# A merge in two half passes, one product drawn ahead of the second half, and the output rows split half by half

## The reference, cut to what matters

```python
merged = jax.nn.sigmoid(g_a) * y_a + jax.nn.sigmoid(g_b) * y_b
x = layer_norm(ALPHA * x + merged @ w_out[i], ln2_g[i], ln2_b[i])
x = layer_norm(ALPHA * x + 0.5 * swiglu(x, ffn2_w1[i], ffn2_w3[i], ffn2_w2[i]),
               ln3_g[i], ln3_b[i])
...
cat = jnp.concatenate([ya * jax.nn.silu(za), yb * jax.nn.silu(zb),
                       yc * jax.nn.silu(zc), yd * jax.nn.silu(zd)], axis=-1)
return jnp.einsum('bte,ed->btd', cat, lp['w_out']), h_final
```

## Time and profile before

| | us |
|---|---|
| median of three runs | 3362.88 (3362.01 to 3364.14) |
| the profiled execution, its own time | 3362.1 |
| its span in the profile | 3360.2 |
| TensorE busy (matmul) | 3260.7 |
| VectorE busy | 1889.2 |
| ScalarE busy | 1087.2 |
| moved by DMA | 249.05 MB, 74 GB/s on average |

### The profile page before, as it was taken

The page is one execution under the profiler, slowest core; times in us unless marked ns, Lnnn a source line. Parts: engine busy times, 40 slices in busy tenths (PEclk is TensorE's granted clock), DMA queues, the critical chain, the costliest instruction groups (busy, mean ns, idle before and its releaser), DMA issues.

```text
span 3360.2 us, 37265 instructions
## 1 busy us (share of the span) xinstructions
PE 3260.7 (97%) x15362; PEld 2649.8 (79%) x15362; DVE 1889.2 (56%) x3223; ACT 1087.2 (32%) x1572; POOL 2.2 (0%) x9
## 2 busy tenths in 40 slices
PE   8999999999999999988989999999999999999898
PEld 7888888877888777777868888888877687788687
DVE  4323323247759678878573332222387698789536
ACT  3121211225242446655142111111155533423412
POOL 0000000000000000000000000000000000000000
PEclk9999999999999999999999999999999999999999
DMA  3211111113333350002201111111111221122141
GB/s 145 84 63 60 66 57 63 63 44 112 106 97 132 129 194 10 7 26 107 106 32 51 51 57 44 51 44 51 51 63 50 94 76 64 44 73 94 69 163 69
DMA packets 88536, 249.05 MB, mean 74 GB/s; under 512 B 8496, under 2 KB 24240, under 8 KB 86832
## 3 DMA queue, kind: packets, MB, share of 16 engines
q1 hardware_dynamic: 88368, 246.68, 21.0%
HBM read 202.60 MB, written 44.04 MB: 73 GB/s over the span
## 4 chain that ended last, share of the span: by engine, by line
PE 88%; DVE 7%; ACT 3%; issue 1%; DMA 0%; DVEq 0%; SPq 0%; ACTq 0%
PE PS L375 87%; PE PS L380 2%; DVE X L1939 1%; DVE WS L1931 1%; DVE HELD L1971 1%; ACT PT L1113 1%; ACT WS L1113 1%; ACT TMP L1540 1%; DVE COLB L2606 0%; DVE PR L1931 0%; DVE XS L1939 0%; DVE PT L1931 0%; DVE HELD L1931 0%; DVE XS L1931 0%; ACT XS L1113 0%
## 5 line engine op out<-in xcount | busy, mean ns | idle before, releaser
L375 PE MATMUL PS<-XS,WS 128*128 128x512 f32 (+1 forms) x8400 | 1943.9, 392 | 21.7 <-DVE XS L1931 13.3
L375 PEld LDWEIGHTS PS<-XS,WS 128*128 128x128 f32 x8400 | 1574.6, 189 | 372.8 <-issue 35.2
L375 PE MATMUL PS<-HS,WS 128*128 128x512 f32 x2208 | 510.3, 391 | 0.7 <-DVE WS L1931 0.7
L375 PEld LDWEIGHTS PS<-HS,WS 128*128 128x128 f32 x2208 | 415.2, 188 | 90.9 <-issue 4.5
L1113 ACT ACTIVATE WS<-RAW 128x1024 fp32r<-128x1024 f32 x286 | 293.5, 1050 | 523.6 <-PE PS L375 461.1
L1931 DVE TENSOR_TENSOR TMP<-TMP,PS 128x512 f32<-128x512 f32 x112 | 76.5, 686 | 651.1 <-PE PS L375 644.4
L1931 DVE TENSOR_TENSOR WS<-RAW,WS 128x1024 fp32r<-128x1024 f32 x286 | 342.8, 1220 | 109.4 <-ACT WS L1113 109.1
L1113 ACT ACTIVATE TMP<-PS 128x512 f32<-128x512 f32 x184 | 109.0, 596 | 524.0 <-PE PS L375 520.4
L1939 DVE SCALAR_TENSOR_TENSOR X<-PS,X 128x512 f32<-128x512 f32 x160 | 109.9, 689 | 240.5 <-PE PS L375 240.2
L1113 ACT ACTIVATE HS<-TMP 128x512 fp32r<-128x512 f32 x88 | 55.6, 632 | 481.4 <-DVE TMP L1931 481.4
L1939 DVE SCALAR_TENSOR_TENSOR CV<-UU,COL,CV 128x1024 f32<-128x1024 f32 x120 | 154.0, 1283 | 3.4
(11 more groups left out here) (294 smaller groups left out, 2786.1 us busy)
## 6 DMA issues: line engine op xcount, KB each, us to landing
RAW<-in_W SPq DMA_DIRECT2D x290, 512.0 KB, 3.6
DC<-TMP SPq DMA_DIRECT2D x32, 256.0 KB, 2.0
X<-in_xT SPq DMA_DIRECT2D x8, 512.0 KB, 8.6
DX<-X SPq DMA_DIRECT2D x2, 2048.0 KB, 8.2
DCZ<-CA SPq DMA_DIRECT2D x8, 512.0 KB, 4.0
DGA<-TMP SPq DMA_DIRECT2D x16, 256.0 KB, 2.6
DGB<-TMP SPq DMA_DIRECT2D x16, 256.0 KB, 3.6
CZ<-DCZ SPq DMA_DIRECT2D x8, 512.0 KB, 6.0
```

The lines of the kernel that those rows point to most:

```text
L375: done = d.matmul(out, l, r, start=first, stop=last)
```

## The change

Merge: the eight rows of h = 0 come first, then the eight of h = 1 in the order 3, 4, 5, 6, 7, 0, 1, 2. Rows 3 to 7 keep their slots; rows 0, 1 and 2 are loaded and split a second time, so the list W has three units more (293 for 290) and the numbers in `loads(...)` rise by three.

Feed-forward: the first product of fi = 2, its w1 for h = 0, is made before the second half of fi = 0 and 1. Its unit takes the fifth slot.

Outputs: rows are split in halves of 512, the first half as soon as the zc product (3, 0) is done; the two rows that come by DMA come in two DMAs of 512 KB. In `c_norm` the squares' second product with ones comes one product earlier, both roots stand together (two table loads fewer) and so do both silu and copy steps.

```diff
+MERGE = [(m, 0) for m in range(8)] + [(m, 1) for m in (3, 4, 5, 6, 7, 0, 1, 2)]
...
+    def ab_row(k, h):
+
+        return RW[:, k, half(h)] if k < 6 else XSf[:, 1, k, half(h)]
...
-            def up(fis):
-                us = {fi: (w.take(), w.take()) for fi in fis}
+            def up(fis, ahead=None, done=None):
+
+                us = {fi: (w.take() if done is None else done, w.take()) for fi in fis}
+                one_more = None
...
+                        early = done is not None and h == 0
+                        if not early:
+                            banks.take(use1, (ac, name, "silu", fi, h))
...
+                        if not early:
+                            product8(us[fi][0], h, use1, tag, within=first)
...
+                    if ahead and h == 0:
+                        one_more, use1 = w.take(), (name, "up1", ahead, 0)
+                        banks.take(use1, (ac, name, "silu", ahead, 0))
+                        product8(one_more, 0, use1, tag, within=None)
+                return one_more
...
-                product8(u, h, use, "mh", pair=mh_pair, beside=h == 1, within=m in (3, 5) and h == 1 or None)
...
+                product8(u, h, use, "mh", pair=mh_pair, beside=h == 1, within=m in (3, 6) and h == 1 or None)
+            us = [w.take() for _ in range(8)]
+            us += us[3:] + [w.take() for _ in range(3)]
+            for i, (u, (m, h)) in enumerate(zip(us, MERGE)):
+                if i == 8:
                     side = merge_norm(0)
+                out_product(u, m, h)
+                if u not in us[i + 1:]:
+                    release(u)
             flush()
             side = merge_norm(1)
...
                     act(ZC[:, m, half(h)], bank("zc", m, h), ACT.Silu).then_inc(*ac.inc("zc", m, h))
+                    if m == 3:
+                        cat_rows(h)
                 release(u)
+
+        def cat_rows(h):
+
+            for k in range(8):
+                e.wait_ge(dma("rw")("rw"), mm("zc", 3, h), *([dma(f"rows{h}")("rows")] if k > 5 else ()))
+                act(XS[:, 0, k, half(h)], ab_row(k, h), ACT.Copy).then_inc(*ac.inc("xs", "ab", k, h))
...
+                u = w.take()
+                if m < 3:
+                    release(u)
+            for h in range(2):
+                for k in range(8):
+                    e.wait_ge(ac("xs", "ab", k, h))
+                    low(XS[:, 1, k, half(h)], ab_row(k, h), XS[:, 0, k, half(h)]).then_inc(*ve.inc("xs", "ab", k, h))
+            release(u)
...
             squared(0)
-            for _ in range(3):
+            yield
+            yield
+            squared(1)
+            for h in range(2):
+                root("c", h, 512, LN_EPS, mm("sq", "c", h, 3))
                 yield
-            squared(1)
-            scaled(0)
-            for _ in range(2):
+            for h in range(2):
+                scaled(h)
                 yield
-            scaled(1)
-            yield
...
-        e.wait_ge(*[cat_in(row, h) for row in (6, 7) for h in range(2)], mm("zc", 3, 1))
-        d.dma_start(XSf[:, 1, 6:8, :], DC[6:8].rearrange("k p n -> p k n")).then_inc(*dma("rows0").inc("rows"))
+        for h in range(2):
+            e.wait_ge(cat_in(6, h), cat_in(7, h), mm("zc", 3, h))
+            d.dma_start(XSf[:, 1, 6:8, half(h)], DC[6:8].rearrange("k p n -> p k n")[:, :, half(h)]).then_inc(
+                *dma(f"rows{h}").inc("rows"))
...
-    w += [(u, "split") for u in by_m(i["w_out"][0])]
+    w_out = by_m(i["w_out"][0])
+    w += [(u, "split") for u in w_out + w_out[:3]]
```

More of the change, by code:

```diff
@@ L496, in ffn @@
             for fi in range(22):
-                if fi != 1:
-                    up([0, 1] if fi == 0 else [fi])
+                if fi == 0:
+                    more = up([0, 1], ahead=None if with_mod else 2)
+                elif fi > 1:
+                    up([fi], done=more if fi == 2 else None)
                 if with_mod and fi:
@@ L1595, in merge @@
             nonlocal side
-            for m in range(3):
-                release(w.take())
-            us = [w.take() for _ in range(5)]
+            us = [w.take() for _ in range(8)]
+            us += us[3:] + [w.take() for _ in range(3)]
+            for u in us[:3]:
+                release(u)
             side = norm("ln2", 0, mm("ya", 7, 1))
-            for m in range(3, 8):
-                hook()
-                release(us[m - 3])
+            for i, u in enumerate(us[8:]):
+                if i in (0, 1, 3, 4, 5):
+                    hook()
+                release(u)
             flush()
@@ L1819, in scaled @@
                 for k in range(4):
-                    e.wait_ge(ac("cs", h, k), ve("xs", "ab", 5, 0))
+                    e.wait_ge(ac("cs", h, k), ve("xs", "ab", 5, 1))
                     act(CVH[:, k, half(h)], CV[:, k, half(h)], ACT.Copy).then_inc(*ac.inc("csh", h, k))
             squared(0)
-            for _ in range(3):
+            yield
[3 more added lines that the diff above has]
+                root("c", h, 512, LN_EPS, mm("sq", "c", h, 3))
                 yield
-            squared(1)
-            scaled(0)
-            for _ in range(2):
+            for h in range(2):
+                scaled(h)
                 yield
-            scaled(1)
-            yield
         def outputs():
             nonlocal side
[L1835 to L1841, removed]
             def ab_pass(ms):
@@ L2692, in out_product @@
                 stt(x, x, ALPHA, bank("wo", m, h), ALU.mult, ALU.add).then_inc(*ve.inc("wo", m, h))
[L2693 to L2703, removed]
-                for _ in range((2, 0, 1, 1, 1)[m - 3]):
+                order = [k for k, g in MERGE if g == h]
+                norm_add("ln2", order.index(m), h, XA, x_now, ve("cxy", 7), order)
+            us = [w.take() for _ in range(8)]
+            us += us[3:] + [w.take() for _ in range(3)]
+            for i, (u, (m, h)) in enumerate(zip(us, MERGE)):
+                if i == 8:
+                    side = norm("ln2", 0, XA, x_now)
+                for _ in range((2, 0, 0, 1, 1, 1, 0, 0)[i - 8] if h else 0):
                     hook()
-                out_product(m, 1)
-                release(us[m - 3])
+                out_product(m, h)
+                if u not in us[i + 1:]:
+                    release(u)
             flush()
@@ L3015, in outputs @@
             x_in = {}
-            for k in range(8):
-                x = RW[:, k, :] if k < 6 else XSf[:, 1, k, :]
-                e.wait_ge(ac("xs", "ab", k, 0))
-                low(XS[:, 1, k, :], x, XS[:, 0, k, :]).then_inc(*ve.inc("xs", "ab", k, 0))
-                ve.same("xs", "ab", k, 1)
             def gated_add(use):
@@ L3360, in sync @@
             x_back(k)
-        loads(277)
+        loads(280)
         for m in range(4):
@@ L3365, in sync @@
             if m % 2:
-                loads(278 + m // 2)
-        loads(282)
+                loads(281 + m // 2)
+        loads(285)
         e.wait_ge(ve("cp", 3, 1))
@@ L3370, in sync @@
             x_back(k)
-        e.wait_ge(*[cat_in(12 + k, h) for k in range(4) for h in range(2)], ac("xs", "ab", 5, 0), ve("xs", "ab", 5, 0))
+        e.wait_ge(*[cat_in(12 + k, h) for k in range(4) for h in range(2)], ac("xs", "ab", 5, 1), ve("xs", "ab", 5, 1))
         d.dma_start(ACf[:, 1], DC[12:16].rearrange("k p n -> p k n")).then_inc(*dma("sg").inc("sg"))
-        loads(286)
+        loads(289)
         e.wait_ge(*[cat_in(8 + k, h) for k in range(4) for h in range(2)], mm("ab", 4, 1))
         d.dma_start(XSf[:, 1, 0:4, :], DC[8:12].rearrange("k p n -> p k n")).then_inc(*dma("rows2").inc("rows"))
-        loads(290)
+        loads(293)
         for p in range(3):
```

33 lines of the change are left out of this document (10 added, 23 removed).

## The result

The changed kernel takes **3330.69 us** (median of 4 runs, 3330.51 to 3333.28), the kernel before, beside it on the same chip, 3363.51. The ratio is 0.9905, 95% interval 0.9888 to 0.9922: 32.8 us less, with some 26 to 38 inside the interval. The forecast was 3330.8, from a kernel before at 3362.88. The profiled execution's span is 3328.7 us, 31.5 less than before's.

The account below looks back on a forecast made before the run. TensorE, 88% of the last-ending chain, was taken as the bound, losing time to idleness and a slower clock. Gains of 16.2 (seam) and 15.9 us (outputs) sum to 32.1, off the median 3362.88: forecast 3330.8 us, range 3326 to 3341.

Parts of the forecast that it names:

- Where the time is: Seam and start of outputs: TensorE waits for VectorE, 8.4 and 4.5 us, then 4.1 and 6.2 us.
- Seam, gain 16.2: Seam of merge and second feed-forward: 10.7 us earlier, with one product of 5.44 us already done.
- of the loss 2.6 stays: Seam: of the 18.8 us lost there before, 2.6 us would remain after the change.
- the prediction's sign: Seam: up1(0, 1) would wait for XS row by row, 2 to 3 us in all.
- The clock taken as full: Seam: the sub-microsecond gaps between rows k would not lower TensorE's clock; cost chosen as 0 us.
- The bound of 2.1: Seam: if the short gaps between rows counted as idleness, the end would be 2.1 us later.
- Outputs, gain 15.9: Start of the outputs: half rows and the norm's new order would save 15.9 of 16.3 us lost.
- the two losses: Time lost before the change: 18.8 us at the seam, 16.3 us at the outputs; 34.9 together.
- Rows late: Outputs: second half's rows land 3 us late beside loads of X, plus clock; time 3336; chance 0.13.
- VectorE the bound at the seam: Seam: VectorE, with 0.3 us to spare, becomes the bound, costing 5 to 9 us; time 3338; chance 0.09.
- Only one place pays: Seam or outputs: the change at one doesn't work or its wait returns; time 3347; chance 0.05.
- Weights set the merge's pace: Merge, first pass: reloads queue behind XA, which would have to be 47 us late; time 3370; chance 0.02.

Follow-up runs that it names:

- e3: The changed kernel with the merge back in its old order, product drawn ahead and new outputs kept: 3339.60 us.
- e2: The changed kernel without the feed-forward product drawn ahead: 3336.90 us.
- e5: The changed kernel with A's and B's rows split whole and one 1 MB transfer, c's norm in its new order: 3337.78 us.
- e4: The changed kernel with the norm of c back in its old order on all three engines, half rows kept: 3339.50 us.
- e6: The changed kernel with six more repeated weight splits on VectorE ahead of the sum of h = 1: 3338.89 us.
- e7: The changed kernel with the remaining norm steps of h = 1 moved ahead of up(1,0)'s silu and product on ScalarE and VectorE: 3328.63 us.
- e1: The changed kernel with merge and second feed-forward as before the change, only the outputs new: 3345.43 us.
- e8: The changed kernel with the outputs as before the change, only merge and second feed-forward new: 3348.70 us.
- e9: The changed kernel itself, unaltered, measured again on another chip: 3332.15 us, against 3361.91 for the kernel before.
- e10: The norm-first kernel (remaining norm steps of h = 1 ahead of up(1,0)'s silu and product) measured again beside the changed kernel: 3329.83 us.

## Why the prediction was right

The time came within 0.1 us of the forecast and each place within 0.6 of its term; that the whole is closer than its parts is luck. The traces show 31.3 us saved where the sum has 32.1, the kernel before measured 3363.51 here and not 3362.88, and the same two kernels on another chip gave 3332.15 and a difference of 29.8 instead of 32.8.

- **Where the time is.** Two places, four waits for VectorE: right. Each of the four has been brought back or kept alone (8.3 in e3, 4.5 in e2, 4.1 in e5, 6.2 in e4), and beyond its idle time each cost 1.6 to 3.0 us more, most of it for the clock.
- **Seam, gain 16.2.** Measured 15.7 from the mean to the row behind up3(0, 1), 15.6 up to zc's last silu, with either outputs. The steps: VectorE at the mean of h = 0, 1675.57 for 1675.7; the sum of h = 1 ready 1719.47 for 1719.6; TensorE there 1719.85 for 1719.9; the margin 0.38 for 0.3; the chain of h = 1 32.5 long, as said, ended at 1753.41 for 1753.5. The reciprocal of h = 0 waited 0.21 us for ScalarE where 0.4 was allowed. Oversized by half a us: of "of the loss 2.6 stays" the size was 3.1 (18.8 - 15.7); up3(0, 1) came 10.45 earlier, not 10.7, from a mean that was 0.15 earlier too. The waits between rows k (0.56, 0.39, 0.40) hold 1.35 of the 3.1, where the prediction's sign was 2 to 3 us of them; the rest isn't placed.
- **The clock taken as full.** Right: 1.00 in each window, with gaps of 0.18, 0.56, 0.39 and 0.40. The bound of 2.1, which would have followed from the Trainium skill (TensorE: Matmul & The Clock Gate, What's actually happening) if gaps so short counted as idleness, wasn't needed. That the throttled state comes back where activity stops agrees with e2, where the same place with a wait of 4.51 shows 0.70 behind it; behind a wait of 3.0 us, told of in the last section, it came back in half of the traces.
- **Outputs, gain 15.9.** Measured 15.7 to 16.2 by the stretches. The half rows took ScalarE 3.22 us for six (0.54 each) and VectorE 3.70 (0.62), as reckoned. The wait for TMP was 0.24, within 0.2 to 0.4. A mis-sized term is the landing of half a MB: 4.1 us, not 3.5. ScalarE did wait for both, in its timeline:

```profile
3112.54 1.15 ACT L1124 ACTIVATE XS<-XSf 128x512 fp32r<-128x512 f32 x2 [0.32 <-DMA XSf<-DC]
3113.94 0.60 ACT L1124 ACTIVATE ZC<-PS 128x512 f32<-128x512 f32 x1 [0.25 <-PE PS L380]
...
3118.16 1.15 ACT L1124 ACTIVATE XS<-XSf 128x512 fp32r<-128x512 f32 x2 [0.51 <-DMA XSf<-DC]
```

  TensorE waited for neither itself, but the second left its mark. The copy of a weight stands behind it on ScalarE, VectorE's split of that weight waited 0.17 us for it, and from there VectorE's queue has no gap up to the squares' sum: 0.17 of TensorE's 0.24. The rule on the fixed part of a DMA that the rival cited (the Trainium skill, DMA: Bandwidth & Descriptors, Anatomy of one DMA) agrees in kind only: two halves take 4.1 us each against 4.8 for the whole in e5, where its formula, an estimate for another path of issue, gives 3.2 and 4.4. The measured times decide.
- **Slips of the sum.** The outputs' work is 43.5 + 3.5 - 0.2 = 46.8 us, not 46.9, and the two losses make 35.1, not 34.9. Neither moves the forecast or its range by more than 0.2.
- **What the sum didn't say.** It gave the outputs one number over two cures. The text followed the new order of the norm of c in its times ("the second squares are summed by about 3151") but never priced it. That is how the expectations of e4 and e5, written later, could be wrong by 7 and 6 us while the prediction held: a total that comes out right doesn't say which part carries it.
- **The rivals.** Rows late: they were, by 0.3 and 0.5 us, and at most 0.17 of it reached TensorE. VectorE the bound at the seam: at the mean it misses that by 0.38 us, as e6 shows (behind the mean its chain is the bound, as e2 and e7 show), and the tally that left out its waits for ScalarE missed nothing large. Only one place pays: no (e1, e8). Weights set the merge's pace: no wait for WS at the seam.

## What to carry to other kernels

Price a change wait by wait, not place by place: ask of each wait which instruction stands ahead of the late one in its engine's queue, and take that part out alone before crediting it. When work moves to another half or another order, the small sums that another engine waits for (here three additions of 2.3 us in all) should go ahead of the long step of the half before them. And an edit of 2 us can be told by a stretch between two events of the trace where whole times spread by 2 to 4, as long as no wait of several us lies in the stretch: behind such a wait the clock can differ between executions.

## What the runs showed of the hardware

**TensorE's clock behind four waits.** Windows right behind four waits of TensorE: 4.51 us (e2), 4.12 (e5), 6.18 (e4), 7.06 (e6), one fence a kernel, and PEclk the third number from the end:

```profile
1748.30:1754.00 5.70, 5.69 (x18) 4.04 (x19) 3.27 (x5) 2.05 (x3) 0.00 (x0) 0.70 0.00 0
```
```profile
3120.50:3126.00 5.50, 5.31 (x15) 3.68 (x15) 5.50 (x6) 5.05 (x6) 0.00 (x0) 0.69 1.03 418
```
```profile
3150.90:3157.00 6.10, 6.08 (x13) 4.18 (x14) 3.87 (x2) 1.98 (x2) 0.00 (x0) 0.51 0.01 3
```
```profile
1727.30:1733.00 5.70, 5.67 (x11) 3.81 (x12) 4.64 (x7) 2.11 (x4) 0.00 (x0) 0.50 0.48 175
```

In each the window after it shows 0.98 to 1.00 again. 0.50 is 1.2 GHz of the two levels, 0.70 a stretch part at 1.2 and part at 2.4. What each kernel lost beyond its added waits was 1.65 us in e2 (5.6 less 3.95), 2.5 in e5 (7.0 less 4.5), 3.0 in e4 (9.3 less 6.3) and 2.1 in e6 (8.2 less 6.1): the price isn't proportional to the wait. Nor does one wait have one price: the same 6.16 us cost 0.6 more in e8 than in before. The gaps of up to 0.56 in the change stand beside a clock of 1.00.

**The same wait, another clock.** Nine traces with the new merge reach its first mean between 1672.81 and 1677.16 us, though nothing ahead of it differs; e2 and e7, on one chip, lie 4.0 apart. In the four whose waits up to there were compared, TensorE's waits differ by a us or two, one way and the other. A part of the spread is the clock. Between 800 and 900 us the change's first trace has 1.00, its second (e9) 0.98, with TensorE busy 97.0 us in both and 397 matmuls against 390. By windows of 4 us all of it lies behind one wait that both have, in TensorE's timelines and the windows behind it, first the first trace, then e9:

```profile
843.88 2.84 PE L380 MATMUL PS<-TMP,ones 128*128 128x512 f32 x6 [3.04 <-ACT TMP L1124]
844.00:848.00 4.00, 4.00 (x13) 2.29 (x14) 3.59 (x13) 2.84 (x4) 0.00 (x0) 1.00 0.35 147
```
```profile
843.38 4.33 PE L380 MATMUL PS<-TMP,ones 128*128 128x512 f32 x6 [3.03 <-ACT TMP L1124]
844.00:848.00 4.00, 4.00 (x8) 1.68 (x7) 3.62 (x11) 1.90 (x3) 0.00 (x0) 0.57 0.23 98
```

The six products behind the wait take 4.33 us in place of 2.84. All twelve traces of this case have this wait, of 3.03 or 3.04 us. In six the six products take 2.84 us (the change, e1, e2, e3, e6, e8), in the other six 4.33 to 4.54 (before, e4, e5, e7, e9, e10). So after a wait of 3.0 us the clock fell in half of the executions, at a cost of 1.5 to 1.7 us, and neither the edit nor the chip decides it: e2 and e7 ran on one chip, e8 and e9 on another. What decides it stays open.
